# Gate sums and running maxima of four mLSTM heads, put on all partitions through a DRAM scratch instead of by TensorE

## The chip, the cores and the metric

One Trainium2 chip, one core. The metric is the device time in microseconds of one execution of the whole kernel. All times on the left of a timeline row count from the start of the profiled span.

## What is computed

The kernel is one decoder layer on 256 tokens of width 2048: a token mixer (four mLSTM heads of dimension 256 beside eight attention heads of dimension 128), an output projection, and a mixture of 32 experts. The change touches the decay matrix of the mLSTM alone. With `b` the running sum of the log forget gates, `i` the input gate, and one chunk over all 256 tokens (which gives the same result as the reference's chunks of 64):

```python
b = jnp.cumsum(fc, axis=-1)
dlog = b[..., :, None] - b[..., None, :] + ic[..., None, :]
dlog = jnp.where(causal, dlog, -jnp.inf)
mt = jnp.maximum(inter, jnp.max(dlog, axis=-1))
dmat = jnp.exp(dlog - mt[..., None])
s = jnp.einsum('bhtd,bhsd->bhts', qc, kc) * dmat
```

The kernel writes `aa[s] = i[s] - b[s]`, and `negM[t] = -max(0, max over s <= t of aa[s])`. Then `dlog - mt` is `aa[s] + negM[t]`. Both are made with the token on the partition, four numbers (one per head) for each token. To take a maximum over `s` for every `t`, each partition needs the row of all 256 `aa` of a head; and to build the decay matrix with `s` on the partition, each partition needs the row of all 256 `negM`.

## The kernel before

Every large matrix product runs in the same way. The weights stream in from DRAM in halves of 8 x 128 rows by 256 columns (1024 KB) into one of four buffers `wraw` (SP, L427, each load waiting until the half four back has been split). ACT rounds a half to fp32r (`round_half`, L673 to L678, which waits for the load and until TensorE has used the half two back), DVE subtracts to get the low part (`split_half`, L1374 to L1378), and TensorE multiplies (`half`, L990), waiting for `split`. There are only two buffers `wsplit`, so the round and the split of a half must fit within the time in which TensorE works on the half before it. DVE also sums the two result columns of every unit of two halves (`sum_halves`), and counts `acc_free`.

The units come in this order: query and key of the mLSTM (channel form), query and key of the attention (QKA), value and output gate of the mLSTM (VO, four pairs of units, each of four halves), value of the attention (VA, two pairs), then the branch gates, two pairs of units for each of four passes of a loop over heads. In each pass TensorE puts the head's small products (L1067 to L1078) between the first half and the second.

What the change touches, all of it in an order written out by hand for each engine:

- Gate sums. `aa` is ready (`aa_ready`, L1513) before VO starts. TensorE turns it to four rows with two transposes before the last pair of VO (L1043 to L1046). DVE copies the rows to `aaT` in SBUF (L1532). After VO, TensorE multiplies `pick[:, h]`, a 0/1 matrix with 4 rows, by `aaT` for each head (L1049 to L1053), which leaves the row of each head on all 128 partitions in PSUM banks 4 and 5. During VA, DVE adds the mask and takes the maxima (L1537 to L1548).
- Running maxima. After VA, TensorE turns `negM` (L1055 to L1058), DVE copies it (L1553), and in each pass over the heads TensorE spreads the head's row with one 0/1 matmul (L1077, L1078). DVE reads it from PSUM bank 7 for the argument of the decay (L1572 to L1575). GpSimd copies the head's 0/1 matrix into `pick_now` (L632).
- ACT in that stretch runs the loop of VO's rounds (L738 to L741), the sigmoid of the output gate (L744, after VO's last sum), five rounds of VA, the exponential of `expm` (L749), the last round of VA (L750), and then the loop over the heads (L753).

Of the kernel before, what the change touches and what calls it, by code (L numbers as in the profile page):

```python
# [136 lines left out]
def layer(nc, x, norm1_g, w_in, conv_w, if_bias, mnorm_g, w_branch_m, w_branch_a, w_out, rel_bias,  # L137
          norm2_g, w_grp, b_grp, w_exp, b_exp, w1, w3, w2, final_g, onehot, out):
    ctx = ExitStack()
    with ctx:  # L140
# [11 lines left out]
        def sem(name):  # L152
            return ctx.enter_context(nc.semaphore(name))
# [50 lines left out]
        pick = sb("pick", [M_HEADS, M_HEADS, P])  # L204
# [7 lines left out]
        aaT = negMT = sb("row_by_head", [M_HEADS, T])  # L212
        negM = sb("negM", [P, TT, M_HEADS])
        pick_now = sb("pick_now", [M_HEADS, P])
        bn = sb("bn", [P, TT, 6])
        mean_var = sb("mean_var", [P, TT, 2])
        expm = sb("expm", [P, TT, M_HEADS])
        AT_CONV = place["at"]
# [83 lines left out]
        rev_dram = nc.dram_tensor("rev_dram", (A_HEADS, REV), F32, kind="Internal").ap()  # L302

# [18 lines left out]
        aa_turned, aaT_ready, aa_spread, negM_ready, negM_turned, negMT_ready, mt_ready, expm_ready = (  # L322
            sem(n) for n in ("aa_turned", "aaT_ready", "aa_spread", "negM_ready", "negM_turned",
                             "negMT_ready", "mt_ready", "expm_ready"))
# [267 lines left out]
        def _(pool):  # L592
# [9 lines left out]
            for m in (before, mask_ts, mask_st, pick):  # L602
                last = pool.memset(m[:], 0.0)
# [11 lines left out]
            choose(mask_st, ALU.is_ge, MASKED, 0, [[1, P]], -1)  # L615
            choose(pick, ALU.not_equal, 1.0, 0, [[-1, M_HEADS], [0, P]], 1).then_inc(consts, 1)
# [11 lines left out]
            with steps.loop(0, M_HEADS, 1) as i:  # L628
# [3 lines left out]
                pool.tensor_copy(pick_now[:], pick[:, ds(i, 1)])  # L632
# [29 lines left out]
        def _(act):  # L662
# [79 lines left out]

            act.wait_ge(acc_free, UNIT_VA)
            act.activation(tok[:, 1], tok[:, 1], ACT.Sigmoid).then_inc(o_ready, 1)  # L744
            for u in range(UNITS_VA - 1):
                round_ahead(u % 2, UNIT_VA, u // 2)
            round_one(UNIT_VA, 4, UNITS_VA // 2 - 1)
            act.wait_ge(mt_ready, 1)
            act.activation(expm[:], expm[:], ACT.Exp, scale=-1.0).then_inc(expm_ready, 1)  # L749
            round_one(UNIT_VA, 5, UNITS_VA // 2 - 1)  # L750

# [169 lines left out]
        def _(pe):  # L921
# [120 lines left out]
            stage(token_half, UNIT_VO, 0, UNITS_VO - 2)  # L1042
            pe.wait_ge(aa_ready, 1)  # L1043
            for t in range(TT):
                last = pe.transpose(ps[0:M_HEADS, 6, t * P:(t + 1) * P], aa[:, t], ident[:])
            last.then_inc(aa_turned, 1)  # L1046
            stage_pair(token_half, UNIT_VO, UNITS_VO // 2 - 1)

            pe.wait_ge(aaT_ready, 1)  # L1049
            for h in range(M_HEADS):  # L1050
                last = pe.matmul(ps[:, 4 + h // 2, (h % 2) * T:(h % 2 + 1) * T], pick[:, h], aaT[:],
                                 start=True, stop=True)
            last.then_inc(aa_spread, 1)  # L1053
            stage(token_half, UNIT_VA, 0, UNITS_VA)
            pe.wait_ge(negM_ready, 1)  # L1055
            for t in range(TT):
                last = pe.transpose(ps[0:M_HEADS, 7, t * P:(t + 1) * P], negM[:, t], ident[:])
            last.then_inc(negM_turned, 1)  # L1058
            with pe.Fori(0, M_HEADS) as i:
# [311 lines left out]
        def _(dve):  # L1371
# [157 lines left out]
            with dve.Fori(0, UNITS_VO // 2 - 1) as i:  # L1529
# [7 lines left out]
            dve.wait_ge(aa_spread, 1)  # L1537
# [515 lines left out]
```

## Time and profile before

| | |
|---|---|
| median of 3 runs | 1224.23 us (1222.94 to 1224.79) |
| span of the profiled execution | 1221.7 us; the difference to the median, 2.5 us, lies outside the span |
| TensorE matmul, weight load | 1186.5 us (97%), 891.8 us (73%) |
| VectorE, ScalarE, GpSimd | 699.4 us (57%), 372.3 us (30%), 44.5 us (4%) |
| DRAM read | 333.93 MB, 275 GB/s over the span |

Up to some 760 us TensorE is busy in every slice and the DMA engines are about 60% busy; from there to the end the experts' weights stream at 430 GB/s with the DMA engines full. Weight halves take 5.1 us from issue to landing. In a timeline a row gives the start, the duration, the engine, the line and the operation; what stands in square brackets is how long the engine had been idle and what ended that. Matmuls overlap one another, so the distance between starts says what one costs, not the duration.

### The profile page before, as it was taken

How to read it: one execution, taken by the hardware profiler on the slowest of the kernel's cores; microseconds unless marked ns; L12 is line 12 of the kernel's file. 1: busy time of each engine (PE TensorE's matmuls, PEld its weight loads, DVE VectorE, ACT ScalarE, POOL GpSimd, SP SyncE). 2: the span in 40 equal slices, each digit the busy share in tenths (PEclk: the TensorE clock that was granted, in tenths of full speed). 3: DMA queues.
4: the chain of work that ended last, by engine and by line, in shares of the span. 5: the costliest groups of instructions: out<-in, count | busy, mean ns of one | idle time of the engine just before them, and what ended most of it. 6: DMA issues, size and time to landing. Idle time of an engine off the chain costs nothing.

```text
span 1221.7 us, 18891 instructions
## 1 busy us (share of the span) xinstructions
PE 1186.5 (97%) x7274; PEld 891.8 (73%) x7274; DVE 699.4 (57%) x1028; ACT 372.3 (30%) x392; POOL 44.5 (4%) x59
## 2 busy tenths in 40 slices
PE   9999999999999999999999999999999999999996
PEld 8888888888888888888898888555455454545552
DVE  5778455554666667666886656444344444343445
ACT  5444433334344354534343442110001110000012
POOL 1000000001002020100000000000000000000002
PEclk9999999999999999999999999999999999999998
DMA  8665665655555554556577595899999999999996
GB/s 298 190 196 186 190 186 174 194 182 172 172 172 168 160 160 152 159 165 201 178 265 187 176 374 212 324 427 430 427 432 432 431 430 432 432 431 430 427 418 251
DMA packets 156827, 336.64 MB, mean 276 GB/s; under 512 B 11232, under 2 KB 135280, under 8 KB 143088
## 3 DMA queue, kind: packets, MB, share of 16 engines
q1 hardware_dynamic: 152208, 335.69, 74.2%
q10 hardware_dynamic: 4576, 0.37, 0.3%
q8 instruction: 29, 0.48, 0.2%
q14 instruction: 14, 0.11, 0.0%
HBM read 333.93 MB, written 2.11 MB: 275 GB/s over the span
## 4 chain that ended last, share of the span: by engine, by line
PE 81%; DMA 14%; SPq 2%; DVE 2%; issue 1%; POOL 1%; ACT 0%; POOLq 0%; DVEq 0%; ACTq 0%
PE ps L955 20%; PE ps L1257 13%; DMA w_b<-in_w_dram 13%; PE ps L984 12%; PE ps L957 10%; PE ps L986 6%; PE ps L1127 4%; PE ps L1287 4%; PE ps L1128 2%; SPq L574 2%; PE ps L1296 1%; PE ps L1211 1%; PE ps L1297 1%; DMA fin_g<-in_final_g_dram 1%; PE ps L930 1%
## 5 line engine op out<-in xcount | busy, mean ns | idle before, releaser
L1377 DVE TENSOR_TENSOR wsplit<-wraw,wsplit 128x2048 fp32r<-128x2048 f32 x119 | 274.8, 2309 | 180.7 <-ACT wsplit L678 180.0
L955 PE MATMUL ps<-act_split,wsplit 128*128 128x512 f32 x1024 | 361.2, 398 | 0.0
L678 ACT ACTIVATE wsplit<-wraw 128x2048 fp32r<-128x2048 f32 x119 | 228.1, 1917 | 382.3 <-PE ps L957 199.0
L957 PE MATMUL ps<-act_split,wsplit 128*128 128x256 f32 x1024 | 286.0, 279 | 0.0
L1257 PE MATMUL ps<-w_a,xe_a 128*64 128x256 f32 x960 | 221.4, 387 | 13.9 <-DMA w_b<-in_w_dram 13.8
L955 PEld LDWEIGHTS ps<-act_split,wsplit 128*128 128x128 f32 x1024 | 192.2, 188 | 47.4 <-issue 1.8
L1257 PE MATMUL ps<-w_b,xe_b 128*64 128x256 f32 x960 | 221.4, 387 | 0.0
L984 PE MATMUL ps<-wsplit,act_split 128*128 128x512 f32 x608 | 217.8, 402 | 0.0
L1257 PEld LDWEIGHTS ps<-w_a,xe_a 128*64 128x64 f32 x960 | 130.5, 139 | 100.8 <-DMA w_b<-in_w_dram 20.4
L957 PEld LDWEIGHTS ps<-act_split,wsplit 128*128 128x128 f32 x1024 | 193.0, 188 | 0.2
L986 PE MATMUL ps<-wsplit,act_split 128*128 128x256 f32 x608 | 171.2, 282 | 0.0
L984 PEld LDWEIGHTS ps<-wsplit,act_split 128*128 128x128 f32 x608 | 114.9, 189 | 30.5 <-issue 2.3
L1257 PEld LDWEIGHTS ps<-w_b,xe_b 128*64 128x64 f32 x960 | 130.5, 139 | 0.0
L986 PEld LDWEIGHTS ps<-wsplit,act_split 128*128 128x128 f32 x608 | 115.6, 190 | 0.0
L1287 PE MATMUL ps<-w_a,hidT 128*64 128x512 f32 x256 | 113.5, 595 | 0.6 <-ACT hidT L869 0.6
L1287 PE MATMUL ps<-w_b,hidT 128*64 128x512 f32 x256 | 113.5, 596 | 0.0
L1934 DVE TENSOR_TENSOR x<-x,ps 128x512 f32<-128x512 f32 x120 | 77.1, 684 | 41.5 <-PE ps L1297 41.4
L1287 PEld LDWEIGHTS ps<-w_a,hidT 128*64 128x64 f32 x256 | 33.7, 137 | 70.0 <-issue 67.9
L1127 PE MATMUL ps<-br_split,wsplit 128*128 128x512 f32 x224 | 77.7, 394 | 0.0
L1128 PE MATMUL ps<-br_split,wsplit 128*128 128x256 f32 x256 | 71.1, 278 | 0.0
L875 ACT ACTIVATE ys_hi<-ps 128x1024 fp32r<-128x1024 f32 (+1 forms) x34 | 33.1, 974 | 110.7 <-PE ps L1287 110.7
L1912 DVE SCALAR_TENSOR_TENSOR hid<-ps,slot_both,sg 128x256 f32<-128x256 f32 x16 | 10.9, 681 | 94.0 <-PE ps L1257 88.0
(315 smaller groups left out, 1133.0 us busy)
## 6 DMA issues: line engine op xcount, KB each, us to landing
wraw<-in_w_in_dram SPq DMA_DIRECT2D x88, 1024.0 KB, 5.1
w_a<-in_w_dram SPq DMA_DIRECT2D x37, 2048.0 KB, 15.5
w_b<-in_w_dram SPq DMA_DIRECT2D x37, 2048.0 KB, 19.5
wraw<-in_w_out_dram SPq DMA_DIRECT2D x16, 1024.0 KB, 5.2
w_a<-in_w_dram SPq DMA_DIRECT2D x14, 1024.0 KB, 12.2
w_b<-in_w_dram SPq DMA_DIRECT2D x14, 1024.0 KB, 15.2
wraw<-in_w_branch_m_dram SPq DMA_DIRECT2D x8, 1024.0 KB, 5.2
wraw<-in_w_branch_a_dram SPq DMA_DIRECT2D x8, 1024.0 KB, 5.1
```

Source lines behind the costliest of these rows:

```text
L678: act.activation(wsplit[:, q % 2, :, 0], wraw[:, q % RAW], ACT.Copy).then_inc(rounded, 1)
L875: act.activation(ys_hi[:, n * 512:end * 512], ps[:, 2 + n:2 + end].rearrange("p a n -> p (a n)"), ACT.Copy).then_inc(ys_rounded, 1)
L955: pe.matmul(banks[b], w[:, k, 0, b * P:(b + 1) * P], a, start=first and k == 0, stop=False)
L957: last = pe.matmul(banks[b][:, 0:T], w[:, k, 1, b * P:(b + 1) * P], a[:, 0], start=False, stop=last_half and k == HALF_K - 1)
L984: pe.matmul(banks[t], a[:, 0, t * P:(t + 1) * P], w[:, k], start=first and k == 0, stop=False)
L986: last = pe.matmul(banks[t][:, 0:UNIT], a[:, 1, t * P:(t + 1) * P], w[:, k, 0], start=False, stop=last_half and k == HALF_K - 1)
L1127: pe.matmul(bank, hi, a, start=k == 0, stop=False)
L1128: last = pe.matmul(bank[:, 0:T], lo, a[:, 0], start=False, stop=k == HALF_K - 1)
L1257: last = pe.matmul(ps[b * SLOTS:(b + 1) * SLOTS, 2 * w, 0:FF], operands[b][:, k], w13[b][:, w, k], start=k == 0, stop=k == DC - 1)
L1287: last = pe.matmul(ps[b * SLOTS:(b + 1) * SLOTS, 2 + n], hidT[:, f, b * SLOTS:(b + 1) * SLOTS], w2s[slot][b][:, f, n * 512:(n + 1) * 512], ...
L1377: dve.tensor_tensor(wsplit[:, q % 2, :, 1], wraw[:, q % RAW], wsplit[:, q % 2, :, 0].bitcast(F32), ALU.subtract).then_inc(split, 1)
L1934: dve.tensor_tensor(cols, cols, ps[:, 6 + g % 2], ALU.add).then_inc(added, 1)
```

## The change

The rows of `aa`, and later those of `negM`, are put on all partitions by DMAs through a small tensor in DRAM. Two stores (one for each half of the tokens) write the 4 x 128 values of 4 bytes, each to its own place, so that a head's 256 values lie in a row; one load then reads the four rows (4 KB) onto each of 128 partitions (512 KB) in `head_rows`, a new tile in SBUF. All of it is issued by ACT, which waits for both stores before it issues the load. The load of `negM` overwrites that of `aa`. DVE waits for the first load before the mask and the maxima, for the second before the loop over the heads, and reads SBUF where it read PSUM. Gone are `pick`, `pick_now`, both pairs of transposes, both copies by DVE, and the eight 0/1 matmuls.

```diff
@@ scalar @@
+            def store_rows(n, by_token, ready):
+
+                act.wait_ge(ready, 1)
+                for t in range(TT):
+                    act.dma_start(bass.AP(tensor=rows_dram.tensor, offset=n * M_HEADS * T + t * P, ap=[[1, P], [T, M_HEADS]]),
+                                  by_token[:, t], allow_slow_non_contiguous=True).then_inc(rows_stored, 16)
+
+            def load_rows(n):
+
+                act.wait_ge(rows_stored, 16 * TT * (n + 1))
+                act.dma_start(head_rows[:].rearrange("p h t -> p (h t)"),
+                              bass.AP(tensor=rows_dram.tensor, offset=n * M_HEADS * T,
+                                      ap=[[0, P], [1, M_HEADS * T]])).then_inc(rows_loaded, 16)
+
+            store_rows(0, aa, aa_ready)
             act.wait_ge(acc_free, UNIT_VA)
             act.activation(tok[:, 1], tok[:, 1], ACT.Sigmoid).then_inc(o_ready, 1)
+            load_rows(0)
             for u in range(UNITS_VA - 1):
                 round_ahead(u % 2, UNIT_VA, u // 2)
             round_one(UNIT_VA, 4, UNITS_VA // 2 - 1)
             act.wait_ge(mt_ready, 1)
             act.activation(expm[:], expm[:], ACT.Exp, scale=-1.0).then_inc(expm_ready, 1)
+            store_rows(1, negM, negM_ready)
             round_one(UNIT_VA, 5, UNITS_VA // 2 - 1)
+            load_rows(1)
...
@@ tensor @@
-            stage(token_half, UNIT_VO, 0, UNITS_VO - 2)
-            pe.wait_ge(aa_ready, 1)
-            for t in range(TT):
-                last = pe.transpose(ps[0:M_HEADS, 6, t * P:(t + 1) * P], aa[:, t], ident[:])
-            last.then_inc(aa_turned, 1)
-            stage_pair(token_half, UNIT_VO, UNITS_VO // 2 - 1)
-
-            pe.wait_ge(aaT_ready, 1)
-            for h in range(M_HEADS):
-                last = pe.matmul(ps[:, 4 + h // 2, (h % 2) * T:(h % 2 + 1) * T], pick[:, h], aaT[:],
-                                 start=True, stop=True)
-            last.then_inc(aa_spread, 1)
+            stage(token_half, UNIT_VO, 0, UNITS_VO)
             stage(token_half, UNIT_VA, 0, UNITS_VA)
-            pe.wait_ge(negM_ready, 1)
-            for t in range(TT):
-                last = pe.transpose(ps[0:M_HEADS, 7, t * P:(t + 1) * P], negM[:, t], ident[:])
-            last.then_inc(negM_turned, 1)
...
                 for k in range(2):
-                    pe.matmul(ps[:, 6, T:REV], qk_now[:, 2 + k, P:T], qk_now[:, k, P:T], start=k == 0, stop=k == 1)
-                pe.wait_ge(negMT_ready, 1)
-                pe.matmul(ps[:, 7, 0:T], pick_now[:], negMT[:], start=True, stop=True).then_inc(scores, 1)
+                    last = pe.matmul(ps[:, 6, T:REV], qk_now[:, 2 + k, P:T], qk_now[:, k, P:T], start=k == 0, stop=k == 1)
+                last.then_inc(scores, 1)
...
@@ vector @@
-            dve.wait_ge(aa_turned, 1)
-            dve.tensor_copy(aaT[:], ps[0:M_HEADS, 6, 0:T]).then_inc(aaT_ready, 1)
-            vo_pair(UNITS_VO // 2 - 1)
             token_unit(UNIT_VA, 0, 0, 2 * TT * M_WIDTH)
 
 
-            dve.wait_ge(aa_spread, 1)
+            dve.wait_ge(rows_loaded, 16)
...
             token_unit(UNIT_VA, 1, 1, 2 * UNIT + 2 * TT * M_WIDTH)
-            dve.wait_ge(negM_turned, 1)
-            dve.tensor_copy(negMT[:], ps[0:M_HEADS, 7, 0:T]).then_inc(negMT_ready, 1)
+            dve.wait_ge(rows_loaded, 16 * 2)
             dve.wait_ge(expm_ready, 1)
...
```

TensorE between VO and VA, before the change (L984 and L986 are the two matmuls of `token_half`, L1051 the 0/1 matmuls):

```order
L986 MATMUL ps<-wsplit,act_split 128x256
L1051 MATMUL ps<-row_by_head,pick 128x256 [waits aaT_ready]
L1051 MATMUL ps<-row_by_head,pick 128x256 x3
L1003 UNCONDITIONAL_BRANCH
L1003 ISA
L994 ISA [waits split]
L984 MATMUL ps<-wsplit,act_split 128x512 [waits acc_free]
```

After the change the four products are gone, and the loop of VO is followed by that of VA.

TensorE in the loop over the heads, between the first half of the gates and the second, before the change:

```order
L1070 MATMUL ps<-qk_now 128x128
L1071 MATMUL ps<-qk_now 128x256
L1074 MATMUL ps<-qk_now 128x256 x2
L1076 MATMUL ps<-qk_now 128x128 x2
L1078 MATMUL ps<-row_by_head,pick_now 128x256 [waits negMT_ready]
L992 REGISTER_ALU
L955 MATMUL ps<-act_split,wsplit 128x512 [waits split]
```

After the change L1078 is missing and `scores` is counted by the product before it.

ACT from the loop of VO's rounds to the first of VA's own, as the change has it (L674 is the round, L678 before; L743 the store, L749 the load of the rows; L755 the sigmoid):

```order
L735 COMPARE_AND_BRANCH
L743 DMA rows_dram<-aa 128x4x1 [waits aa_ready]
L743 DMA rows_dram<-aa 128x4x1
L755 ACT_TABLE_LOAD
L755 ACTIVATE tok<-tok 128x2048 [waits acc_free]
L749 DMA head_rows<-rows_dram 128x1024 [waits head_rows_stored]
L674 ACTIVATE wsplit<-wraw 128x8x256 [waits used,raw_loaded2]
```

Before the change only the table load, the sigmoid and the rounds stood there; the wait for the stores now stands ahead of the round of VA's third half.

ACT at the end of VA, as the change has it (L761 is the exponential of `expm`, L775 that of the decay):

```order
L761 ACT_TABLE_LOAD
L761 ACTIVATE expm<-expm 128x8 [waits mt_ready]
L743 DMA rows_dram<-negM 128x4x1 [waits negM_ready]
L743 DMA rows_dram<-negM 128x4x1
L674 ACTIVATE wsplit<-wraw 128x8x256 [waits used,raw_loaded1]
L749 DMA head_rows<-rows_dram 128x1024 [waits head_rows_stored]
L767 UNCONDITIONAL_BRANCH
L767 ISA
L673 ISA [waits raw_loaded2]
L674 ACT_TABLE_LOAD
L674 ACTIVATE wsplit<-wraw 128x8x256 [waits used]
L774 REGISTER_ALU
```

The three DMAs are new there, and the wait for the stores stands ahead of the round of the gates' third half.

## Rows read from the trace of the kernel before

**Rows 1.** The page's busy times, and TensorE's waits (total us, times, longest).
```profile
PE 1186.5 (97%) x7274; PEld 891.8 (73%) x7274; DVE 699.4 (57%) x1028; ACT 372.3 (30%) x392; POOL 44.5 (4%) x59
...
PE ps L1257 <- DMA w_b<-in_w_dram: 13.8, 8, 2.6
```

**Rows 2.** Stretches: us, busy of PE, PEld, DVE, ACT, POOL, PEclk, DMA share, GB/s.
```profile
295.00:299.00 4.00, 4.00 (x14) 3.43 (x15) 2.34 (x1) 3.21 (x3) 3.68 (x2) 0.57 0.45 141
...
341.00:560.00 219.00, 219.00 (x1261) 191.09 (x1260) 145.60 (x237) 97.65 (x102) 24.80 (x23) 1.00 0.53 163
...
800.00:1000.00 200.00, 194.70 (x1324) 105.74 (x1322) 87.35 (x166) 20.73 (x29) 0.00 (x0) 0.99 1.01 431
```

**Rows 3.** SP's own waits: its DMA queue.
```profile
SPq L427 <- DVE wsplit L1377: 596.8, 113, 9.1
...
SPq L450 <- DMA rev_dram<-rev: 4.4, 1, 4.4
```

**Rows 4.** Timeline of TensorE about the transposes of `aa`.
```profile
269.96 0.28 PE L986 MATMUL ps<-wsplit,act_split 128*128 128x256 f32 x1
270.07 0.38 PE L1045 MATMUL ps<-ident,aa 128*4 128x128 f32 x2
...
270.53 0.28 PE L986 MATMUL ps<-wsplit,act_split 128*128 128x256 f32 x1
```

**Rows 5.** Timeline of TensorE between VO and VA, and in VA's first half.
```profile
292.79 0.28 PE L986 MATMUL ps<-wsplit,act_split 128*128 128x256 f32 x1
293.00 1.99 PE L1051 MATMUL ps<-row_by_head,pick 4*128 4x256 f32 x8
294.92 0.50 PE L984 MATMUL ps<-wsplit,act_split 128*128 128x512 f32 x1
...
299.02 0.40 PE L984 MATMUL ps<-wsplit,act_split 128*128 128x512 f32 x1
```

**Rows 6.** Timeline of TensorE in the first pass over the heads.
```profile
350.33 0.69 PE L1078 MATMUL ps<-row_by_head,pick_now 4*128 4x256 f32 x2
350.96 0.50 PE L955 MATMUL ps<-act_split,wsplit 128*128 128x512 f32 x1
```

**Rows 7.** Timeline of ACT from the last rounds of VO's loop into VA.
```profile
293.10 1.91 ACT L678 ACTIVATE wsplit<-wraw 128x2048 fp32r<-128x2048 f32 x1 [3.73 <-PE ps L986]
...
296.32 1.91 ACT L744 ACTIVATE tok<-tok 128x2048 f32<-128x2048 f32 x1
302.44 1.92 ACT L678 ACTIVATE wsplit<-wraw 128x2048 fp32r<-128x2048 f32 x1 [4.20 <-PE ps L986]
308.10 1.92 ACT L678 ACTIVATE wsplit<-wraw 128x2048 fp32r<-128x2048 f32 x1 [3.75 <-PE ps L986]
```

**Rows 8.** Timeline of DVE: a split in VA, then the maxima and the first head.
```profile
304.39 2.29 DVE L1377 TENSOR_TENSOR wsplit<-wraw,wsplit 128x2048 fp32r<-128x2048 f32 x1 [7.00 <-ACT wsplit L678]
...
336.96 0.17 DVE L1548 TENSOR_SCALAR negM<-negM 128x8 f32<-128x8 f32 x1
...
349.77 2.29 DVE L1377 TENSOR_TENSOR wsplit<-wraw,wsplit 128x2048 fp32r<-128x2048 f32 x1 [3.19 <-ACT wsplit L678]
...
358.86 2.29 DVE L1377 TENSOR_TENSOR wsplit<-wraw,wsplit 128x2048 fp32r<-128x2048 f32 x1 [0.55 <-ACT wsplit L678]
```

**Rows 9.** Timeline of ACT at the end of VA.
```profile
339.59 0.21 ACT L749 ACTIVATE expm<-expm 128x8 f32<-128x8 f32 x1
...
347.82 1.91 ACT L678 ACTIVATE wsplit<-wraw 128x2048 fp32r<-128x2048 f32 x1 [2.59 <-PE ps L957]
```

**Rows 10.** The page's DMA issues (KB each, median us from issue to landing).
```profile
wif_raw<-in_w_in_dram SPq DMA_DIRECT2D x1, 64.0 KB, 9.1
...
bias_at<-rev_dram SPq DMA_DIRECT2D x8, 128.0 KB, 3.0
...
fin_g<-in_final_g_dram SPq DMA_DIRECT2D x1, 1024.0 KB, 12.2
```

**Rows 11.** Timeline of ACT's queue: the issue of a load in small pieces.
```profile
645.76 0.40 ACTq L808 DMA_DIRECT2D wrt<-in_w_grp_dram  x1
```

More of the change, by code:

```diff
@@ L201, in layer @@
         AT_PHASE = place["at"]
-        pick = sb("pick", [M_HEADS, M_HEADS, P])
         ifb = sb("ifb", [P, 2 * M_HEADS])
@@ L211, in layer @@
         aa = sb("aa", [P, TT, M_HEADS])
-        aaT = negMT = sb("row_by_head", [M_HEADS, T])
         negM = sb("negM", [P, TT, M_HEADS])
-        pick_now = sb("pick_now", [M_HEADS, P])
         bn = sb("bn", [P, TT, 6])
@@ L217, in layer @@
         expm = sb("expm", [P, TT, M_HEADS])
+        head_rows = sb("head_rows", [P, M_HEADS, T])
         AT_CONV = place["at"]
@@ L302, in layer @@
         rev_dram = nc.dram_tensor("rev_dram", (A_HEADS, REV), F32, kind="Internal").ap()
+        rows_dram = nc.dram_tensor("rows_dram", (2, M_HEADS, T), F32, kind="Internal").ap()
         x_loaded = [sem("x_loaded_0"), sem("x_loaded_1")]
@@ L321, in layer @@
                              "ls_ready", "cum_summed", "aa_ready"))
-        aa_turned, aaT_ready, aa_spread, negM_ready, negM_turned, negMT_ready, mt_ready, expm_ready = (
-            sem(n) for n in ("aa_turned", "aaT_ready", "aa_spread", "negM_ready", "negM_turned",
-                             "negMT_ready", "mt_ready", "expm_ready"))
+        negM_ready, mt_ready, expm_ready, rows_stored, rows_loaded = (
+            sem(n) for n in ("negM_ready", "mt_ready", "expm_ready", "head_rows_stored", "head_rows_loaded"))
         o_ready, staged = sem("o_sigmoid_ready"), sem("staged")
@@ L601, in _ @@
                                pattern=[[-1, P]], channel_multiplier=1).then_inc(ident_ready, 1)
-            for m in (before, mask_ts, mask_st, pick):
+            for m in (before, mask_ts, mask_st):
                 last = pool.memset(m[:], 0.0)
@@ L614, in _ @@
             choose(mask_ts, ALU.is_ge, MASKED, 0, [[-1, P]], 1)
-            choose(mask_st, ALU.is_ge, MASKED, 0, [[1, P]], -1)
-            choose(pick, ALU.not_equal, 1.0, 0, [[-1, M_HEADS], [0, P]], 1).then_inc(consts, 1)
+            choose(mask_st, ALU.is_ge, MASKED, 0, [[1, P]], -1).then_inc(consts, 1)
             def root(col, n, turn):
@@ L631, in _ @@
                 pool.wait_ge(ha_summed, i * 2 + 1)
-                pool.tensor_copy(pick_now[:], pick[:, ds(i, 1)])
                 pool.tensor_copy(qk_now[:, 0:4], qk[:, ds(i * 4, 4)])
@@ L1527, in vo_pair @@
                     token_unit(UNIT_VO, i, u, (i // 2) * (TT * M_WIDTH) + (i % 2) * (2 * UNIT))
-            with dve.Fori(0, UNITS_VO // 2 - 1) as i:
+            with dve.Fori(0, UNITS_VO // 2) as i:
                 vo_pair(i)
-            dve.wait_ge(aa_turned, 1)
-            dve.tensor_copy(aaT[:], ps[0:M_HEADS, 6, 0:T]).then_inc(aaT_ready, 1)
-            vo_pair(UNITS_VO // 2 - 1)
             token_unit(UNIT_VA, 0, 0, 2 * TT * M_WIDTH)
-            dve.wait_ge(aa_spread, 1)
+            dve.wait_ge(rows_loaded, 16)
             mask_2 = mask_ts[:].unsqueeze(1).to_broadcast([P, 2, P])
@@ L1540, in _ @@
                 token_unit(UNIT_VA, n, 1 - n, n * 2 * UNIT + 2 * TT * M_WIDTH)
-                rows = ps[:, 4 + n].rearrange("p (h s) -> p h s", h=2)
+                rows = head_rows[:, 2 * n:2 * n + 2]
                 dve.tensor_tensor(prob[:, :, 0:P], rows[:, :, 0:P], mask_2, ALU.add)
@@ L1571, in _ @@
                 dve.wait_ge(scores, i + 1)
-                dve.scalar_tensor_tensor(decay[:, 0:P], ps[:, 7, 0:P], aa[:, 0, ds(i, 1)], mask_st[:], ALU.add, ALU.add)
-                dve.tensor_scalar(decay[:, P:T], ps[:, 7, P:T], aa[:, 0, ds(i, 1)], None, ALU.add)
-                dve.scalar_tensor_tensor(decay[:, T:REV], ps[:, 7, P:T], aa[:, 1, ds(i, 1)], mask_st[:],
+                row = head_rows[:, ds(i, 1)].rearrange("p h t -> p (h t)")
+                dve.scalar_tensor_tensor(decay[:, 0:P], row[:, 0:P], aa[:, 0, ds(i, 1)], mask_st[:], ALU.add, ALU.add)
+                dve.tensor_scalar(decay[:, P:T], row[:, P:T], aa[:, 0, ds(i, 1)], None, ALU.add)
+                dve.scalar_tensor_tensor(decay[:, T:REV], row[:, P:T], aa[:, 1, ds(i, 1)], mask_st[:],
                                          ALU.add, ALU.add).then_inc(decay_arg, 1)
```

## The prediction

> **What bounds the kernel now.** I read the page's busy times first: TensorE has work in 97% of the span, and its only wait of any size, 13.8 us in eight pieces, is in the experts' stage [rows 1]. The stretches confirm it for the region of the change: from 341 to 560 us TensorE is busy all 219 us, while the DMA engines are half idle [rows 2]. So until the experts begin, whatever TensorE no longer executes comes off the time, as long as nothing keeps it waiting instead. In the experts' stage the DMA engines are full (share 1.01, 431 GB/s) [rows 2]. That stage can't get shorter, but it starts when TensorE is done, since SP's loads wait for buffers that the splits release, 596.8 us in all [rows 3]: it should move forward whole. Last I read the timelines of TensorE, ACT and DVE about the places of the edit, for what each removed product costs and how much room each new wait has.
>
> **What is removed.** One pair of matmuls of a half (128x512 and 128x256) takes 0.354 us from start to start: two rounds, each set off by the end of a half of 16 pairs, lie 308.10 - 302.44 = 5.66 us apart [rows 7].
> - Transposes of `aa`: from one L986 to the next 0.57 us instead of 0.354, so 0.22 us [rows 4]. Those of `negM` have the same form and count: 0.22 us.
> - The four products of L1051: from L986 at 292.79 to L984 at 294.92 is 2.13 us where 0.12 us is the step between two matmuls without them (270.07 - 269.96 = 0.11), so 2.0 us [rows 4, 5].
> - A fall of the clock behind them. The granted clock was 0.57 on the mean between 295 and 299 us, that is, mostly the 1.2 GHz level, and 1.00 in the heads' stretch [rows 2]. TensorE had just spent 1.99 us on products with 4 rows out of 128. From 294.92 to 299.02 it did 7 pairs in 4.10 us [rows 5] where 7 x 0.354 = 2.48 us were due: 1.6 us lost. I take it that the 4-row products brought the fall about and that it goes with them. The Trainium skill (TensorE: Matmul & The Clock Gate, "What's actually happening") says the clock is gated by how busy TensorE has been lately. TensorE counts as busy in this trace just before the fall, so by that rule as I read it the products aren't the cause; this is a rival below.
> - L1078, four times: 350.96 - 350.33 = 0.63 us each, 2.5 us in all [rows 6]. There was no fall of the clock in that stretch (1.00) [rows 2], so nothing more is to be had there.
>
> Together 0.22 + 0.22 + 2.0 + 1.6 + 2.5 = 6.5 us. DVE's two copies, GpSimd's copies of `pick_now`, and reading SBUF for PSUM I cost at nothing: DVE is busy 57% and GpSimd 4% [rows 1], and TensorE waits for neither there. That cover stays.
>
> **What is added.** Six DMAs, issued by ACT. An issue takes ACT 0.40 us in the nearest row, a load in pieces of 16 bytes [rows 11]. How long the stores take to land, x, no row shows directly. The lowest bound is 3.0 us (`bias_at`, a load), and the highest in that stage 9.1 us (`wif_raw`, many small pieces queued behind four weight loads); 12.2 us (`fin_g`) was measured with the DMA engines full [rows 10]. The nearest row is the one store to DRAM whose landing is waited for, `rev_dram`: 4.4 us of waiting after an issue of about 0.4, with a weight load in flight [rows 3]. I take x = 4.8 us. The stores here are smaller but consist of 512 single elements each; I keep 3.0 and 9.1 for the range. SP's weight loads share the DMA engines with them, but those are half idle in that stretch [rows 2], and a weight half is asked for four halves ahead (4 x 5.66 = 22.6 us).
>
> *First place, in VA.* All times are on the old clock. VA's first half starts at 293.0 instead of 294.92 and runs at full clock, so it ends at 298.7 and the second at 304.3. The round of the third half could start at 298.7; from the start of a round to the end of its split are 304.39 + 2.29 - 302.44 = 4.24 us [rows 7, 8], so it must start by 304.3 - 4.3 = 300.0 or TensorE waits. On ACT the round that begins at 293.10 ends at 295.0 [rows 7]. Then come the first store at 295.0, the second at 295.4, the table load and the sigmoid to about 299.1 (they ended at 298.2 before), and the wait for the stores: landed at 295.4 + x, the load issued by 295.8 + x. With x = 4.8 that is 300.6, so TensorE waits 0.65 us. In general it waits x - 4.15, and nothing below x = 4.15. DVE needs the loaded rows only two splits later, after 312 us, so the load has over 10 us.
>
> *Second place, before the heads.* `negM` is ready at 337.1 [rows 8], but the stores come behind the exponential, which ends at 339.8 [rows 9]: landed at 340.2 + x = 345.0. ACT meanwhile does VA's last round, issues the load at 345.0 and is free at 345.4, ahead of the gates' third round at 347.82 [rows 9]. The load (512 KB, between a 128 KB load of 3.0 us and a weight half of 5.1) lands about x later, near 350 us. DVE wants it before its split at 349.77 [rows 8]. That split must start by 353.7: TensorE's half between then starts at 350.33 now and ends at 356.0, less 2.3. A delay to 350 costs nothing. TensorE waits 2x - 13.4 us, so only from x = 6.7. The next split, at 358.86 [rows 8], has 1.1 us of room to 362.3 and is itself held by a round that waits for TensorE, so it is late only if DVE's chain is over 2 us late.
>
> **The sum.** -6.5 + 0.65 = -5.85 us against the profiled execution: its span goes from 1221.7 to 1215.9 us. The median of the runs is 2.5 us above that span and nothing of the change lies outside it, so 1224.2 - 5.8 = 1218.4 us. The Trainium skill (DMA: Bandwidth & Descriptors, "Anatomy of one DMA", a fit for GpSimd's queue) has about 2.0 us plus bytes by 436 GB/s. As an estimate that gives 2.0 us for a store and 3.2 for the load, no wait anywhere, and 1217.7 us; the measured store speaks against it.
>
> **Rivals.**
> 1. *The clock's fall stays* (it came from something else at that moment). For it: TensorE was busy throughout; ACT, DVE and GpSimd were all at work there, as nowhere else. Against: it follows right on the 4-row products. Then 6.5 - 1.6 = 4.9 us are won; VA's first half ends 1.6 us later, which gives the late round the 0.65 us it needs, so nothing is given back: 1219.3 us.
> 2. *The stores land late, and ACT's round queue stops behind them* (the side of slower). Mechanism: 1024 elements of 4 bytes, each its own write to DRAM, hold ACT at the wait ahead of a round, and two DMAs in a row hold DVE ahead of the heads. Price: (x - 4.15) + (2x - 13.4) = 3x - 17.5; it eats the 6.5 us at x = 8.0. At x = 9.1 it is 9.8 us, so 1227.5 us; at 12.2 it is 19.1, so 1236.8 us. For it: `wif_raw`, also in small pieces, took 9.1 us [rows 10]. Against: that one had four weight loads ahead of it, and here one at most is in flight (DMA share 0.45 [rows 2]). The Trainium skill (DMA: Bandwidth & Descriptors, "Rules for kernel authors") warns that a non-contiguous last dimension becomes one descriptor per element, and advises against just this form; no row of this case has elements of 4 bytes.
> 3. *The gain doesn't reach the end*: the experts' stage, full in its DMA engines, keeps its time and takes up the lead, or its starts fall badly. About 1224 us. Against it stands that all its first loads wait for buffers of the stage before [rows 3].
>
> **How the numbers follow.** The forecast (x from 3.0 to about 6.5, clock fall gone) gets 0.60: 1217.7 to 1220.2 us before scatter. The clock's fall staying: 0.16. Late stores: 0.13, of which 0.08 end clearly slower and 0.05 near zero. Gain lost later: 0.11, 0.02 of it still faster. What a measurement can tell from no change is about 0.2%, 2.4 us (the three runs spread by 1.85). Faster 0.78, same 0.14, slower 0.08. The range takes in the forecast, rival 1, and late stores up to x = 7.3 (4.4 us of waiting): 1216.6, a run's scatter under the lowest, to 1222.2 us.
>
> **What would show it.** Right: no matmul with 4 rows in the trace; granted clock 1.00 through VA's first half; TensorE idle about 0.65 us once, before VA's third half, ended by a split; none before the gates' third half; stores landing in 4 to 6 us; the first gate half some 4 us earlier, the first load of experts' weights some 6 us earlier. Wrong: an idle time over 3 us at either place, a clock below 1.00 near 295 us, or the experts' stage longer by what was won.

## The result and the profile after

The changed kernel takes 1229.36 us (median of 4 runs, 1228.15 to 1231.21), the kernel before 1224.06 us (4 runs, 1222.94 to 1224.79): 1.0047 times as long, 95% interval 1.0034 to 1.0060, some 5 us slower. The forecast was 1218.4 us with a range up to 1222.2; the time lies outside it, on the other side of the kernel before.

The page and TensorE's waits (total us, times, longest) of the changed kernel; the first line of the waits is the same as in [rows 1], the other two are new:

```profile
span 1226.4 us, 18867 instructions
...
PE 1181.5 (96%) x7254; PEld 888.9 (72%) x7254; DVE 698.1 (57%) x1026; ACT 372.0 (30%) x392; POOL 44.6 (4%) x53
...
q10 hardware_dynamic: 6976, 1.42, 0.6%
...
PE ps L1255 <- DMA w_b<-in_w_dram: 13.8, 8, 2.6
PE ps L998 <- DVE wsplit L1375: 7.8, 1, 7.8
...
PE ps L969 <- DVE wsplit L1375: 1.9, 2, 1.3
```

TensorE does 5.0 us less work and waits 9.7 us more, for splits of DVE, which stand behind ACT's round at the first place and behind the load of the rows at the second. What ACT did there is in its timeline, first about the stores of `aa` (before: [rows 7]), then about those of `negM` (before: [rows 9]):

```profile
293.61 1.93 ACT L674 ACTIVATE wsplit<-wraw 128x2048 fp32r<-128x2048 f32 x1 [3.73 <-PE ps L1000]
293.76 0.97 ACTq L743 DMA_DIRECT2D rows_dram<-aa  x2
...
296.85 1.92 ACT L755 ACTIVATE tok<-tok 128x2048 f32<-128x2048 f32 x1
307.92 0.34 ACTq L749 DMA_DIRECT2D head_rows<-rows_dram  x1
308.37 3.71 ACT L674 ACTIVATE wsplit<-wraw 128x2048 fp32r<-128x2048 f32 x2 [9.60 <-DMA rows_dram<-aa]
...
343.70 0.93 ACTq L743 DMA_DIRECT2D rows_dram<-negM  x2
...
348.34 1.92 ACT L674 ACTIVATE wsplit<-wraw 128x2048 fp32r<-128x2048 f32 x1 [2.21 <-PE ps L1000]
353.61 0.34 ACTq L749 DMA_DIRECT2D head_rows<-rows_dram  x1
```

The stores of `aa` are issued at 293.8 and 294.2 us, and the second has landed at 307.9, 13.7 us after its issue. Meanwhile ACT's sigmoid is over at 298.8 and nothing else may start, though the round of VA's third half has been due since 299.3 (5.65 us behind the round at 293.6). TensorE's timeline shows the price, 7.85 us of idling and then work at the lower clock (before, in the same place: [rows 5]):

```profile
304.60 0.28 PE L1000 MATMUL ps<-wsplit,act_split 128*128 128x256 f32 x1
312.73 0.79 PE L998 MATMUL ps<-wsplit,act_split 128*128 128x512 f32 x1 [7.85 <-DVE wsplit L1375]
```

The stretches of the changed kernel (us, busy of PE, PEld, DVE, ACT, POOL, PEclk, DMA share, GB/s) show two more things:

```profile
298.00:300.00 2.00, 2.00 (x13) 1.73 (x12) 0.00 (x1) 0.77 (x1) 1.36 (x1) 1.00 0.03 3
...
304.00:306.00 2.00, 0.88 (x6) 0.51 (x4) 0.00 (x0) 0.00 (x0) 0.00 (x0) 1.00 0.46 24
306.00:308.00 2.00, 0.00 (x0) 0.00 (x0) 0.00 (x0) 0.00 (x0) 0.00 (x0) 1.00 0.57 66
...
312.00:315.00 3.00, 2.27 (x7) 1.98 (x8) 3.00 (x4) 0.08 (x1) 0.00 (x0) 0.50 0.37 77
```

First, from 298 to 308 us the DMA engines move next to nothing (3 to 66 GB/s) although a weight half, issued at 298.17 us, is in flight beside the 4 KB of `aa`. That half took 13.8 us to land instead of 5.1. Second, after the idle time the granted clock is 0.50, the 1.2 GHz level, which costs about 1.6 us more.

At the second place the longer of TensorE's two waits (1.3 us) is ended by this split, which stands behind the load of the rows (issued at 353.6, landed at 360.8 us):

```profile
360.99 2.29 DVE L1375 TENSOR_TENSOR wsplit<-wraw,wsplit 128x2048 fp32r<-128x2048 f32 x1 [8.40 <-DMA head_rows<-rows_dram]
```

To add up where the time went, one event serves as a mark in all traces: ACT's rounds of the same halves follow TensorE's progress closely. Stretch A is from the round at 270.27 to that at 342.02 us of the kernel before (all of the first place), stretch B from there to the round at 560.83 (all of the heads):

```profile
270.27 1.92 ACT L678 ACTIVATE wsplit<-wraw 128x2048 fp32r<-128x2048 f32 x1 [3.73 <-PE ps L986]
...
342.02 1.92 ACT L678 ACTIVATE wsplit<-wraw 128x2048 fp32r<-128x2048 f32 x1 [2.22 <-PE ps L986]
...
560.83 1.92 ACT L678 ACTIVATE wsplit<-wraw 128x2048 fp32r<-128x2048 f32 x1 [3.63 <-PE ps L1128]
```

In the changed kernel the same rounds start at 271.00, 348.34 and 564.97 us. Stretch A takes 77.3 instead of 71.8 us, stretch B 216.6 instead of 218.8 us: +5.6 and -2.2. The rest of the difference between the spans (4.7 - 3.4 = 1.3 us) had arisen by 0.7 us before the change's first place and by 0.6 us in the experts' stage. The 0.7 us belong to the trace of the kernel before and not to the change: its halves from 45 to 106 us took 5.55 us each, where they took 5.65 in the changed kernel and in every other trace here (see the last section).

### The profile page after: what moved, and what is told of

It is laid out like the page before. It is cut to its first block, busy times and chain, and to the rows that moved or that the text cites. A ratio compares the mean times of both kernels' runs of the same rounds, so it can differ in the third digit from the quotient of the medians.

```text
span 1226.4 us, 18867 instructions
## 1 busy us (share of the span) xinstructions
PE 1181.5 (96%) x7254; PEld 888.9 (72%) x7254; DVE 698.1 (57%) x1026; ACT 372.0 (30%) x392; POOL 44.6 (4%) x53
## 3 DMA queue, kind: packets, MB, share of 16 engines
q10 hardware_dynamic: 6976, 1.42, 0.6%
## 4 chain that ended last, share of the span: by engine, by line
PE 79%; DMA 15%; DVE 2%; SPq 2%; issue 1%; POOL 1%; ACT 1%; DVEq 0%; ACTq 0%; POOLq 0%
PE ps L969 19%; PE ps L1255 14%; DMA w_b<-in_w_dram 11%; PE ps L998 11%; PE ps L971 9%; PE ps L1000 5%; PE ps L1285 4%; PE ps L1125 4%; PE ps L1126 2%; PE ps L1294 2%; SPq L572 1%; PE ps L1209 1%; PE ps L1295 1%; DMA rows_dram<-aa 1%; DMA fin_g<-in_final_g_dram 1%
## 5 line engine op out<-in xcount | busy, mean ns | idle before, releaser
L674 ACT ACTIVATE wsplit<-wraw 128x2048 fp32r<-128x2048 f32 x119 | 228.0, 1917 | 379.7 <-PE ps L971 191.0
L1255 PE MATMUL ps<-w_a,xe_a 128*64 128x256 f32 x960 | 221.0, 387 | 13.9 <-DMA w_b<-in_w_dram 13.8
```

The lines of the kernel that those rows point to most:

```text
L674: act.activation(wsplit[:, q % 2, :, 0], wraw[:, q % RAW], ACT.Copy).then_inc(rounded, 1)
L1255: last = pe.matmul(ps[b * SLOTS:(b + 1) * SLOTS, 2 * w, 0:FF], operands[b][:, k], w13[b][:, w, k], start=k == 0, stop=k == DC - 1)
```

## The experiments

Theory A: the store of a token's values in pieces of 4 bytes is slow by the number of its pieces, and ACT, whose rounds stand behind the wait, hands that on to TensorE. Rivals are named in the expectations. Stretches A and B of all kernels stand in one table. A row with "1 run" has the time of a single run and no interval.

| kernel | stores of `aa`, of `negM` | stretch A | stretch B | span | median, ratio to before (95%) |
|---|---|---|---|---|---|
| before | none | 71.8 | 218.8 | 1221.7 | |
| before, profiled again | none | 70.2 | 219.0 | 1222.2 | 1223.9, 1 run |
| the change | 4 bytes, 4 bytes | 77.3 | 216.6 | 1226.4 | 1229.4, 1.0047 (1.0034 to 1.0060) |
| `e5_negM_only` | none, 4 bytes | 69.4 | 218.7 | 1220.7 | 1222.9, 0.9984 (0.9974 to 0.9994) |
| `e6_aa_only` | 4 bytes, none | 77.4 | 218.8 | 1229.1 | 1231.2, 1.0044 (1.0029 to 1.0060) |
| `e1_early` | 4 bytes early, 4 bytes | 67.9 | 218.8 | 1221.9 | 1220.9, 0.9958 (0.9943 to 0.9974) |
| `e2_packed` | 16 bytes, 16 bytes | 67.9 | 214.1 | 1214.0 | 1215.9, 0.9925 (0.9908 to 0.9942) |
| `e7_packed_early` | 16 bytes early, 16 bytes | 67.9 | 214.1 | 1214.0 | 1217.4, 0.9948 (0.9931 to 0.9964) |
| `e8_eight_bytes` | 8 bytes, 8 bytes | 69.4 | 214.3 | 1216.3 | 1218.0, 1 run |
| `e4_half_late` | 4 bytes, half of them late | 73.8 | 217.1 | 1225.3 | 1227.0, 1 run |
| `e3_spaced` | 4 bytes, 512 bytes apart (see there) | 67.9 | 217.3 | 1219.2 | 1220.9, 1 run |
| `e9_spaced64` | the same, 64 bytes apart | 67.9 | 217.6 | 1220.4 | 1222.1, 1 run |
| `e10_spaced32` | the same, 32 bytes apart | 67.9 | 219.8 | 1221.0 | 1222.7, 1 run |
| `e11_by_head` | 4 bytes, 8 stores | 76.6 | 216.9 | 1227.1 | 1228.8, 1 run |

The lowest values, 67.9 and 214.1, come back in several kernels: they are the stretches with everything removed and nothing waited for. In these traces the waits that the change added, with the slower clock behind them, are thus 77.3 - 67.9 = 9.4 us in A (7.85 of waiting and 1.6 of clock) and 216.6 - 214.1 = 2.5 us in B.

**One part of the change at a time.** `e5_negM_only` leaves `aa` to TensorE, with the lines L1043 to L1053, L1531, L1532 and `rows = ps[:, 4 + n]` of the kernel before. In `e6_aa_only` it is the other way round, with L1055 to L1058, L1077, L1078 and L1552, L1553 of the kernel before. Both also keep some small tiles at other addresses in SBUF.

```diff
             act.activation(expm[:], expm[:], ACT.Exp, scale=-1.0).then_inc(expm_ready, 1)
+            store_rows(negM, negM_ready)
             round_one(UNIT_VA, 5, UNITS_VA // 2 - 1)
+            load_rows()
...
```
```diff
+            store_rows(aa, aa_ready)
             act.wait_ge(acc_free, UNIT_VA)
             act.activation(tok[:, 1], tok[:, 1], ACT.Sigmoid).then_inc(o_ready, 1)
+            load_rows()
...
```

> Only negM goes through the scratch; aa is turned and spread by TensorE as before. Theory A (the time is lost at the first place, where ACT stands at the wait for the stores of aa ahead of a round of VA, and the second place is nearly paid for by the removed products): 1 to 2 us below the kernel before, TensorE's wait in the first pass over the heads about 1.9 us in two pieces, the fall of the clock behind the 4-row products near 295 us back. Rival B (the loss is made mostly before the heads, where stores and load follow one another): 3 us or more above the kernel before.

> Only aa goes through the scratch; negM is turned and spread by TensorE as before. Theory A: TensorE waits about 8 us before VA's third half and runs at half clock for some us after it, so 5 to 6.5 us above the kernel before, more than the whole change. Rival B: at most 2 us above.

Measured: 0.9984 times the time before with `negM` alone (TensorE waits 2.9 us once, not 1.9 in two pieces) and 1.0044 times with `aa` alone (7.6 us once), which isn't more than the 1.0047 of the whole change, as I had expected. The loss sits in the first place, as theory A had it. The second place isn't nearly as good as thought, though: in `e5_negM_only` the removed products (4.7 us in stretch B) are paid back whole by the waits, and what its trace gained lies in stretch A, where seven halves took 5.55 us instead of 5.65, which the edit doesn't explain. One expectation failed outright: the clock didn't fall behind the 4-row products, see below.

**The same stores, earlier.** `e1_early` splits the loop of VO's rounds and issues the stores of `aa` before its last pass.

```diff
-            for unit, start, units in ((UNIT_QKA, 1, UNITS_QKA), (UNIT_VO, 0, UNITS_VO)):
-                with act.Fori(start, units // 2) as i:
+            for unit, start, end in ((UNIT_QKA, 1, UNITS_QKA // 2), (UNIT_VO, 0, 3), (UNIT_VO, 3, UNITS_VO // 2)):
+                if unit == UNIT_VO and start:
+                    store_rows(0, aa, aa_ready)
+                with act.Fori(start, end) as i:
...
-            store_rows(0, aa, aa_ready)
             act.wait_ge(acc_free, UNIT_VA)
```

> The whole change, but ACT issues the two stores of aa one pair of VO earlier (four rounds, 22.6 us), same stores, same loads. Theory A (not the stores' own time but ACT's round standing behind the wait costs): the stores still take 10 to 14 us, TensorE's wait before VA's third half is gone and the clock stays at 1.00 there, 5 to 6 us below the kernel before (about 1218.5). Rival C (the stores slow the machine itself, by keeping the DMA engines from the weight loads): the wait moves with the stores to the last pair of VO, and the time stays above the kernel before.

The DMA issues of `e1_early` from 271 to 290 us (KB each, median us to landing):

```profile
wraw<-in_w_in_dram SPq DMA_DIRECT2D x3, 1024.0 KB, 9.7
rows_dram<-aa ACTq DMA_DIRECT2D x2, 2.0 KB, 12.4
```

The stores are as slow as ever and the weight halves beside them land late too, but nobody waits: halves are asked for 22.6 us ahead. Stretch A falls to 67.9 us, the time to 0.9958 of that before, and rival C is out: the weight halves do suffer, as it said, but TensorE doesn't wait for them. 0.9958 is a gain of 5.1 us; by the medians of the two kernels, 1220.9 and 1224.9 us (15 runs beside these), it is 4.0, short of the 5 to 6 expected. The profiled execution was the slowest of the five and shows that a gain here can be lost later: it was 2.7 us ahead of the first trace of the kernel before at the round of the last weight half (722.0 against 724.7 us), and the rest of it, mainly the experts' stage, took 2.9 us longer, 499.9 against 497.1 us. In the other traces that rest took 497.2 to 500.1 us, 497.9 in the second one of the kernel before. Why it varies stays open.

**The same bytes in fewer pieces.** In `e2_packed` the four values of a token lie side by side.

```diff
-        head_rows = sb("head_rows", [P, M_HEADS, T])
+        head_rows = sb("head_rows", [P, T, M_HEADS])
...
-                    act.dma_start(bass.AP(tensor=rows_dram.tensor, offset=n * M_HEADS * T + t * P, ap=[[1, P], [T, M_HEADS]]),
+                    act.dma_start(bass.AP(tensor=rows_dram.tensor, offset=n * M_HEADS * T + t * P * M_HEADS, ap=[[M_HEADS, P], [1, M_HEADS]]),
...
-                rows = head_rows[:, 2 * n:2 * n + 2]
+                rows = head_rows[:, :, 2 * n:2 * n + 2].rearrange("p t h -> p h t")
...
-                row = head_rows[:, ds(i, 1)].rearrange("p h t -> p (h t)")
+                row = head_rows[:, :, ds(i, 1)].rearrange("p t h -> p (t h)")
```

> The whole change at its places, but a token's four values lie side by side in the scratch: each store is 128 pieces of 16 bytes instead of 512 of 4 bytes, the same bytes; DVE reads the rows with a stride. Theory A1 (a store's time goes with the number of pieces): landing falls from 8 to 14 us to 3 to 5.5 us, TensorE's wait before VA's third half under 1.5 us, 4 to 6.5 us below the kernel before. Rival D (a store to DRAM beside the weight loads takes that long whatever its pieces): landing and time as in the change, some 5 us above the kernel before.

The page's line of ACT's DMA queue (packets, MB, share) and, from 290 to 300 us, the DMA issues (KB each, median us to landing) of `e2_packed`:

```profile
q10 hardware_dynamic: 5440, 1.42, 0.5%
...
wraw<-in_w_in_dram SPq DMA_DIRECT2D x2, 1024.0 KB, 6.0
head_rows<-rows_dram ACTq DMA_DIRECT2D x1, 512.0 KB, 5.2
rows_dram<-aa ACTq DMA_DIRECT2D x2, 2.0 KB, 3.8
```

The stores landed in 3.8 us, TensorE waited in neither place, and the time is 0.9925 of that before, 9.0 us less by the medians (1215.9 against 1224.9). Rival D is out. The gain is larger than the 4 to 6.5 us expected; the removed products were worth more than I had counted. But this run changes two things at once, the number of pieces (128 for 512 in a store) and how they lie.

**Number of pieces, or how they lie.** `e3_spaced` is `e1_early` with a second set of stores at the old place, the same 1024 elements of 4 bytes into another scratch, 512 bytes apart. ACT waits for these too.

```diff
+            def store_spaced():
+
+                for t in range(TT):
+                    act.dma_start(bass.AP(tensor=spaced_dram.tensor, offset=t * P * P, ap=[[P, P], [T * P, M_HEADS]]),
+                                  aa[:, t], allow_slow_non_contiguous=True).then_inc(rows_stored, 16)
...
-                act.wait_ge(rows_stored, 16 * TT * (n + 1))
+                act.wait_ge(rows_stored, 16 * TT * (n + 2))
...
+            store_spaced()
             act.wait_ge(acc_free, UNIT_VA)
```

> The stores of aa are made one pair of VO earlier, and at their old place ACT stores the same 1024 elements once more, each of 4 bytes, 512 bytes apart in another scratch, and waits for these as the change does. Theory A1 (a store's time goes with the number of pieces): these stores take 9 to 14 us again and TensorE waits 5 to 9 us before VA's third half. Rival E (small writes to neighbouring addresses hold one another up): the spaced stores land in 3 to 5 us and TensorE doesn't wait.

The DMA issues of `e3_spaced` from 292 to 299 us (KB each, median us to landing), against those of the change from 293 to 307:

```profile
wraw<-in_w_in_dram SPq DMA_DIRECT2D x2, 1024.0 KB, 6.1
...
spaced_dram<-aa ACTq DMA_DIRECT2D x2, 2.0 KB, 4.2
```
```profile
wraw<-in_w_in_dram SPq DMA_DIRECT2D x1, 1024.0 KB, 13.8
rows_dram<-aa ACTq DMA_DIRECT2D x2, 2.0 KB, 13.1
```

As many pieces, of the same size, land in 4.2 instead of 13.1 us. Of the two weight halves in the first fence the one issued at 298.3 us, beside the stores, took 7.2 us; in the change the one issued at 298.2 took 13.8. My theory of the number of pieces falls; rival E stands: small writes to neighbouring addresses hold one another up, and the weight loads with them. The pieces are taken up equally fast in both. In both, all have begun by 298 us. Of the change this is the line of ACT's queue from 293 to 298 us (packets, MB, share); from 298 to 308 us the queue has no packet at all, so those ten us lie behind the start of the pieces:

```profile
q10 hardware_dynamic: 1056, 0.00, 11.9%
```

`e9_spaced64` and `e10_spaced32` put 64 and 32 bytes for the 512 (`[[16, P], [T * 16, M_HEADS]]` and `[[8, P], [T * 8, M_HEADS]]`).

> As the run with stores 512 bytes apart, but 64 bytes apart. Theory E (writes that fall into one and the same small stretch of DRAM hold one another up): with one write in 64 bytes they land in 4 to 5 us, if 64 bytes is the stretch or more than it; if the stretch is 128 bytes or larger, in 5 to 8 us. TensorE's wait before VA's third half is 0 to 1 us in the first case.

> As before, 32 bytes apart. If the stretch is 64 bytes, two writes share one and the landing is a little above that of 64 bytes, 4.5 to 6 us; if it is 32 bytes, the same as at 64 and 512.

Landing took 4.4 us at 64 bytes and 4.6 us at 32 bytes, and stretch A is 67.9 us in both. So pieces 32 bytes apart are nearly free of it. Distances between 4 and 32 bytes weren't tried in this form, so the stretch that matters may also be smaller than 32 bytes. Nor is it shown that it is a matter of one small stretch: 32 bytes apart the pieces are also spread over eight times as many bytes of DRAM.

`e8_eight_bytes` puts the heads in pairs, 256 pieces of 8 bytes in a store, and `e4_half_late` stores two heads a pair of VO earlier and two at the old place, 256 pieces of 4 bytes in a store, adjacent.

```diff
+                    act.dma_start(bass.AP(tensor=rows_dram.tensor, offset=n * M_HEADS * T + t * P * 2, ap=[[2, P], [2 * T, 2], [1, 2]]),
+                                  by_token[:, t].rearrange("p (a b) -> p a b", a=2), allow_slow_non_contiguous=True).then_inc(rows_stored, 16)
...
```
```diff
+                    act.dma_start(bass.AP(tensor=rows_dram.tensor, offset=(n * M_HEADS + first) * T + t * P, ap=[[1, P], [T, 2]]),
+                                  by_token[:, t, first:first + 2], allow_slow_non_contiguous=True).then_inc(rows_stored, 16)
...
```

> Two heads' values side by side in the scratch: each store is 256 pieces of 8 bytes, the same bytes as in the change. Theory A1: landing between that of 128 pieces (2.2 to 5.2 us) and of 512 (8 to 14 us), as with 256 pieces of 4 bytes: 5 to 7 us, a wait of 1 to 3 us before VA's third half. If bytes a piece matter and not their number, it differs from the run with 256 pieces of 4 bytes.

> Two heads of aa are stored one pair of VO earlier, the other two at the old place: two stores of 256 pieces of 4 bytes instead of 512. Theory A1: they land in 5 to 7 us, TensorE waits 1 to 3 us before VA's third half. Rival D (a fixed price for any store of elements): 12 us or more and a wait of 7 us. For negM four stores of 256 pieces stand in place of two of 512: together as slow as before by both.

The stores of `aa` in `e8_eight_bytes`, then those at the old place in `e4_half_late` (KB each, median us to landing):

```profile
rows_dram<-aa ACTq DMA_DIRECT2D x2, 2.0 KB, 6.3
```
```profile
rows_dram<-aa ACTq DMA_DIRECT2D x2, 1.0 KB, 8.6
```

Both stores have 256 pieces. With 8 bytes, four pieces to 32 bytes, they take 6.3 us, as expected, with a wait of 1.3 us; with 4 bytes, eight pieces to 32 bytes, 8.6 us and a wait of 3.7 us, although that is half the data. That is above what theory A1 had for `e4_half_late` (5 to 7 us, 1 to 3 of waiting) and below what rival D had. Taken with the rest, at the same place: at most one piece to 32 bytes 4.2 to 4.6 us (512 pieces), two 3.8 us (128 pieces, `e2_packed`), four 6.3 us (256), eight 8.6 us (256) and 13.1 us (512). What lies beyond some 4 us grows with how many pieces share 32 bytes. That it grows with their number too is less sure. The two early stores of `e4_half_late`, 256 pieces, landed in 9.4 and 12.0 us, where 512 took 11.8 and 13.0 in `e1_early`; and the stores of `negM` in the change, 512 adjacent pieces as well, took 7.9 and 9.5.

`e11_by_head` asks whether the pieces must come from one store. It writes the layout of `e2_packed` in pieces of 4 bytes, one store for each head and half of the tokens, at the old place.

```diff
+                    for h in range(M_HEADS):
+                        act.dma_start(bass.AP(tensor=spaced_dram.tensor, offset=t * P * M_HEADS + h, ap=[[M_HEADS, P], [1, 1]]),
+                                      aa[:, t, h:h + 1], allow_slow_non_contiguous=True).then_inc(rows_stored, 16)
...
```

> At the old place the same 1024 values of 4 bytes go token by token into the layout of the run with 16-byte pieces, as eight stores of 128 pieces (one for each head and half of the tokens), 16 bytes apart; the true stores are made one pair of VO earlier. The eight issues take ACT 3 to 4 us. If writes hold one another up within a stretch whoever makes them, or if their number counts, the last lands 8 us or more after its issue began and TensorE waits 5 us or more. If only writes of different DMA engines into one stretch do, it lands in 4 to 6 us after its issue and TensorE waits 2 to 4 us, for the issues.

The DMA issues from 292 to 312 us:

```profile
spaced_dram<-aa ACTq DMA_DIRECT2D x8, 0.5 KB, 7.6
```

The issues take 3.7 us, the last store (issued at 297.6) lands 9.0 us later, TensorE waits 6.0 us. The first of the eight stores landed in 4.4 us, the second in 6.7, the others in 7.3 to 9.0, and the weight half issued at 298.6 us took 13.7 us, as in the change:

```profile
wraw<-in_w_in_dram SPq DMA_DIRECT2D x1, 1024.0 KB, 13.7
```

In one of these stores two pieces share 32 bytes, in all of them together eight do. So the slowness comes back when the neighbours are written by different stores. That pieces of different stores hold one another up is the likely reading, but eight stores in a row to places far apart weren't tried, so their mere number isn't ruled out. Whether it matters that pieces come from different DMA engines isn't settled by this. The Trainium skill (DMA: Bandwidth & Descriptors, "The descriptor swizzle") gives four neighbouring partitions to one engine in a transfer to 128 partitions. If that holds for a store from 128 partitions too, every 32 bytes here were written by one engine, and it was slow all the same; no trace here shows the engine of a piece.

**Whether anything is left.** `e7_packed_early` joins the edits of `e1_early` and `e2_packed`.

> Pieces of 16 bytes, and the stores of aa one pair of VO earlier. Theory: nothing of the wait is left with 16-byte pieces, so this gives the same as that run, 7 to 10 us below the kernel before; if ACT's wait there still cost something, 1 to 2 us more are won.

The time is 0.9948 of that before (0.9931 to 0.9964), 6.4 us by this ratio and a little under the 7 to 10 expected; the span and both stretches are as in `e2_packed`. Nothing is left to win there, and `e2_packed`, with the smaller edit, is the version to take.

**The clock, and the kernel before once more.** `b0_before_again` is the kernel before, unchanged.

> The kernel before, unchanged, profiled a second time. It tells which features of its trace come back. If the 4-row products bring the fall of the clock about, the granted clock is again near 0.57 from 295 to 299 us; if the fall is chance, this trace has 1.00 there like the run with only negM through the scratch, and the halves from 45 to 106 us take 5.55 or 5.65 us by chance as well.

The same four microseconds of the kernel before in its second profile, and of `e5_negM_only`, which runs the same 4-row products at 294.2 to 296.2 us (columns as above):

```profile
295.00:299.00 4.00, 4.00 (x23) 3.20 (x21) 2.66 (x2) 3.97 (x3) 3.37 (x2) 1.00 0.61 218
```
```profile
296.00:300.00 4.00, 4.00 (x24) 3.40 (x23) 2.34 (x1) 3.44 (x3) 3.91 (x2) 1.00 0.48 153
```

The clock stays at 1.00 in both. The products were there in three traces and the clock fell in one. The four products with the round after them took 9.34 us from round to round with the fall and 7.83 without it, so the fall cost 1.5 us where it occurred. The products don't bring it about by themselves; whether they make it more likely stays open.

## Why the prediction was wrong

It went as the second rival said, "the stores land late, and ACT's round queue stops behind them", which had 0.13. Point by point:

- *What bounds the kernel* held. TensorE's progress carried through: 4.1 of the 4.7 us between the spans of the change and the kernel before are there at the round of the last weight half, 728.81 against 724.68 us. With `e2_packed` 8.4 us gained there come out as 7.7 us of span. So rival 3 isn't what happened in the change. It isn't out for good: in the profiled run of `e1_early` the experts' stage took the whole lead of 2.7 us back.
- *Transposes and products between VO and VA*: 0.22 + 2.0 = 2.2 us; measured 70.2 - 67.9 = 2.3.
- *The fall of the clock*, 1.6 us: right in size (1.5), wrong as a lasting cost. It was read from one execution, and rival 1, that it came from something else, was the better reading. In the changed kernel the clock was 1.00 there and fell after 308 us, within TensorE's idle time.
- *L1078 and the transposes of `negM`*, 2.5 + 0.22 = 2.7 us: measured 218.8 - 214.1 = 4.7 us. I had taken the distance from L1078 to the next matmul. See the last section for the rest.
- *x, the time of a store.* This is the step that failed: "I take x = 4.8 us". It was 13.7 us for the second store of `aa` and about 9.5 us for that of `negM` (issued at 344.1, the load behind it at 353.6). The row it leaned on, `rev_dram`, is a store too, but its pieces aren't single elements side by side. I took the small pieces seriously only as many packets (`wif_raw`), not as writes that meet in the same few bytes. The bounds of 3.0 and 9.1 us weren't bounds: the fastest store of `negM` in `e2_packed` landed in 2.2 us.
- *The room of ACT's round* was found rightly: the wait for the stores ahead of VA's third round. My formula had x - 4.15; the idle time was 13.7 - 5.85 = 7.85 us, because the stores are issued at 293.8, while the round that began at 293.6 still runs, not behind it. I hadn't counted the 1.6 us that the clock takes after the idle time.
- *The second place*: the issue of the stores again doesn't wait for the exponential (343.7 us; the exponential runs at 345.9). Store and load together took 17.1 us, the load 7.2 of it, and DVE's split waited for the load, as predicted. TensorE waited 1.9 us in two pieces and stretch B lost 2.5 us; the remaining 0.6 us I can't place. The same code cost 3.2 to 5.7 us there in other traces (stretch B of `e3_spaced`, `e9_spaced64`, `e1_early`, `e10_spaced32`). Part of that spread is the clock again. In `e5_negM_only`, `e1_early` and `e10_spaced32` TensorE waited once, 2.7 to 3.7 us, and the granted clock fell to the 1.2 GHz level behind the wait; in the others it waited in two pieces and kept 1.00. From 356 to 360 us, `e1_early` and then `e3_spaced` (columns as above):

```profile
356.00:360.00 4.00, 4.00 (x14) 3.42 (x15) 3.93 (x14) 3.45 (x8) 0.00 (x0) 0.57 0.72 218
```
```profile
356.00:360.00 4.00, 4.00 (x24) 3.46 (x23) 3.97 (x9) 3.44 (x9) 0.00 (x0) 1.00 0.78 260
```

- The formula of the rival with each place's own times, (13.7 - 4.15) + (9.5 + 7.2 - 13.4), gives 12.85 us of waiting. Measured are 9.7 us of waiting, and 9.43 + 2.55 = 12.0 us with the slower clock and what I can't place. They ate all 8.6 us that the removed products and the fall give in these two traces, and 3.4 more. That the rival's price at x = 9.1, 1227.5 us, lies near the 1229.4 measured is luck: x was far longer, and the first place gave more room than the formula has.
- The Trainium skill's rule (DMA: Bandwidth & Descriptors, "Rules for kernel authors"), that a non-contiguous last dimension becomes one descriptor per element and is to be rearranged, gave the right advice here: 6976 packets against 5440 in `e2_packed`. Its reason isn't the whole of it, since as many single elements 32 bytes apart land in 4.6 us.

## What to carry to other kernels

A store of single elements that end up side by side in DRAM isn't a small transfer, however few bytes it has: put what one partition writes side by side (16 bytes a piece were enough here), or keep the pieces at least 32 bytes apart, and look at what it does to the big loads in flight. An in-order engine that has work for the bound engine shouldn't stand at a DMA's semaphore; issue the store a round or two earlier and wait late, which alone turned +5.3 us into a gain of 4 to 5. A gain that is read from a single trace, such as a fall of the clock, needs a second one before it goes into a sum.

## What I had not expected of the hardware

Small adjacent writes hold up the loads of others. For 10 us beside 1024 such writes of 4 bytes the traffic stayed at 3 to 66 GB/s, and the weight half in flight took 13.8 us; beside the same writes 512 bytes apart it took 7.2 us.

TensorE has two paces at the same granted clock of 1.00. A half of 16 pairs takes 5.65 or 5.55 us from round to round. Between 45 and 106 us the first trace of the kernel before has 5.55 and the second 5.65, with the same code. Behind the 4-row products ahead of VA both have 5.65, and `e5_negM_only` has 5.55. In the heads it is regular: behind the 0/1 product of L1078 the next two halves have the slower pace in all four passes of both traces, and without it, from the second pass on, the faster one in all of them. The timelines of TensorE in the second pass over the heads, first of the kernel before, then of `e2_packed`:

```profile
401.66 0.61 PE L1076 MATMUL ps<-qk_now 128*128 128x128 f32 x4
402.20 0.69 PE L1078 MATMUL ps<-row_by_head,pick_now 4*128 4x256 f32 x2
402.82 0.50 PE L955 MATMUL ps<-act_split,wsplit 128*128 128x512 f32 x1
```
```profile
396.78 0.61 PE L1075 MATMUL ps<-qk_now 128*128 128x128 f32 x4
397.14 0.48 PE L969 MATMUL ps<-act_split,wsplit 128*128 128x512 f32 x1
```

From the last product before L1078 to the half it is 402.82 - 401.66 = 1.16 us before and 0.36 us without it: 0.80, not the 0.63 I had read off. Some halves behind it then take 5.55 us instead of 5.65, so a pass gains about 1.15 us. What the two paces are, and what switches between them elsewhere, no run here tells.
